# Start addresses of the operands that TensorE streams, in a float32r kernel of three transformer layers

## The chip, the core and the metric

The kernel runs on one core of a Trainium2 chip. The metric is the device time of one execution in microseconds. The median of 3 runs of the kernel before is 2257.28 us (2252.32 to 2262.8).

## The reference

A sequence of 512 positions with 1024 features goes through three residual layers, all in float32: retention with 4 heads and a squared-ReLU MLP of width 4096; attention over chunks of 64 with 16 heads and a relative bias, and a second such MLP; and a hybrid layer. Cut to what matters:

```python
h = h + _retention(rmsnorm(h), ret_w_in, ret_gn_g, ret_w_out)
h = h + relu(rmsnorm(h) @ mlp_w1[0]) ** 2 @ mlp_w2[0]
h = h + _chunk_attention(rmsnorm(h), att_w_in, att_rel_bias, att_w_out)
h = h + relu(rmsnorm(h) @ mlp_w1[1]) ** 2 @ mlp_w2[1]
x = rmsnorm(h)
z = rmsnorm(x) @ w_in            # q, k, v of three attentions, a forget gate, three gates
merged = sigmoid(ga) * (o_a @ w_pa) + sigmoid(gb) * (o_b @ w_pb) + sigmoid(gc) * (o_c @ w_pc)
x = x + merged @ w_o
a, b = split(causal_dwconv(rmsnorm(x) @ w_up))
return rmsnorm(x + (silu(a) * b) @ w_down)
```

Nearly all of the arithmetic is products of the 512 positions with weight matrices.

## The kernel before, in words

Everything is kept feature-major: a tile is 128 features by 512 positions, and the residual `h` is 8 such tiles. The weights come as a stream of 358 units of 128 x 1024 float32 (512 KB each), most of them eight blocks of 128 x 128, in the order in which the products need them. SyncE loads unit after unit into the ring `raw` of four slots. ScalarE rounds a unit to float32r into `w_hi` (line 952), VectorE puts the rest, raw minus w_hi, into `w_lo` (line 1376), both three units ahead of the products. The activations are split likewise: `x_hi` and `x_lo` hold the 8 tiles of a layer's input, and `arena_r`, 29 tiles of 512 float32r, holds every other split operand: q, k, v and probabilities, attention outputs, the MLP's hidden tiles, the products of the gated unit. `arena` holds 17 tiles of plain float32 scratch.

A product of two float32 numbers is made of three float32r products, written in the helper `mm3`, whose three lines are 487, 488 and 489 in the profile:

```python
(lh, ll), (rh, rl) = left, right
pe.matmul(dst, lh, rh, start=start, stop=False, **kw)
pe.matmul(dst, lh, rl, start=False, stop=False, **kw)
return pe.matmul(dst, ll, rh, start=False, stop=stop, **kw)
```

```
tensor            bytes each   before: start, past a multiple of 2048
w_hi, w_lo        16384        32896, 49280     128
x_hi, x_lo        16384        82048, 98432     128
h, rbc, sq, acc, diag          65664 to 127104  128
arena             34816        133952           832
arena_r           59392        168768           832
```

A slice of these that TensorE streams starts a multiple of 512 bytes further on, a whole tile a multiple of 2048.

Of the kernel before, what the change touches and what calls it, by code (L numbers as in the profile page):

```python
# [23 lines left out]
F32R = mybir.dt.float32r  # L24
# [3 lines left out]
P = 128  # L28
S = 512
D = 1024  # L30
KT = D // P
# [4 lines left out]
UNIT = 1024  # L36
RING = 4
# [14 lines left out]

NORMS, BOTH = 7, 4
STRIP = 640

# [5 lines left out]
N_COLS = C_CB + 2 * PAIRS  # L63
# [114 lines left out]
def wait(eng, sem, count):  # L178

    count = lin(count)  # L180
    assert count.b > 0 or not count.a, count.b
    if count.positive():
        eng.wait_ge(sem, count.val())

def build(nc, stream, x_t, cols, wf, f_bias, sinks, rel_pad, rel_2, c_rope, c_decay, c_sq, c_tri, c_sel,
          c_onehot, c_masked, out):

    strips = nc.dram_tensor("bias_strips", (12, P, STRIP), F32, kind="Internal").ap()
    with ExitStack() as ctx:  # L190
        def sb(name, shape, dt=F32):
            return ctx.enter_context(nc.sbuf_tensor(name, shape, dt))
# [2 lines left out]
            return ctx.enter_context(nc.semaphore(name))  # L195

        raw = sb("raw", [P, RING, UNIT])
        w_hi = sb("w_hi", [P, RING, UNIT], F32R)
        w_lo = sb("w_lo", [P, RING, UNIT], F32R)
        h = sb("h", [P, KT, S])  # L200
        x_hi = sb("x_hi", [P, KT, S], F32R)
        x_lo = sb("x_lo", [P, KT, S], F32R)
        rbc = sb("rbc", [P, S])
        sq = sb("sq", [P, 4, S])
        acc = sb("acc", [P, S])
        diag = sb("diag", [P, TT, P])
        ident = sb("ident", [P, P])
        ones = sb("ones", [P, P])
        sqr = sb("sqr", [P, 3, P], F32R)
        colv = sb("colv", [P, N_COLS])  # L210
        small = sb("small", [P, 12, 16])
        wf_raw = sb("wf_raw", [P, KT, 4])
        wf_hi = sb("wf_hi", [P, KT, 4], F32R)
        wf_lo = sb("wf_lo", [P, KT, 4], F32R)
        rel_sb = sb("rel_sb", [BUCKETS + 2, 12])
        arena = sb("arena", [P, 17 * S])
        arena_r = sb("arena_r", [P, 29 * S], F32R)

        banks = [ctx.enter_context(nc.psum_tensor(f"bank{n}", [P, S], F32)) for n in range(8)]

# [175 lines left out]

        onehot_sb = arena[0:BUCKETS + 2, 8 * S:8 * S + STRIP]
        strip_sb = arena[0:12, 10 * S:10 * S + STRIP]
        masks_sb = arena[:, 12 * S:12 * S + 3 * P].rearrange("p (m n) -> p m n", m=3)
# [1518 lines left out]
        def _(pool):  # L1918
# [35 lines left out]
            pool.wait_ge(strip_copied, 1)  # L1954
            pool.dma_start(strips, strip_sb.unsqueeze(1).broadcast_to([12, P, STRIP])).then_inc(strip_saved, 16)

# [44 lines left out]
            def toeplitz(sm, hd, table, row, offset, w):  # L2001

                wait(pool, sm.biased, 4 * (hd - 1) if hd >= 2 else 0)
                src = bass.AP(table.tensor, row * P * STRIP + offset + P - 1, [[STRIP - 1, P], [1, w]])
                pool.dma_start(bias[hd % 2][:, 0:w], src).then_inc(sm.bias[hd % 2], 16)
# [65 lines left out]
def bucket_table():  # L2072

    f = np.float32
    ahead = 511 - np.arange(STRIP)
    dist = np.maximum(ahead, 0)
# [162 lines left out]
```

## Time and profile before

| | before |
|---|---|
| median of 3 runs | 2257.28 us |
| the profiled execution, span from first to last instruction | 2256.0 us |
| TensorE busy | 98% of the span |
| VectorE, ScalarE, GpSimd busy | 53%, 36%, 11% |
| mean granted TensorE clock | 0.983 |

The profiled execution has no time of its own beside its span; the span is 1.3 us under the median of the runs, within their spread. Matmuls are pipelined: one starts before the one before it has ended, so the mean duration of a matmul in the rows is longer than the distance from start to start, and the sum of the groups' times exceeds the span. What one product costs TensorE is to be read from the starts. The clock is given as a share of full speed: 1.0 is the 2.4 GHz level, 0.5 the 1.2 GHz level.

### The profile page before, as it was taken

The page shows a single profiled execution, that of the slowest core. Times are in us where ns is not written, and L with a number is a line of the kernel's source. Part 1 is how long each engine was busy: PE and PEld are TensorE (multiplying, and loading weights), DVE is VectorE, ACT ScalarE, POOL GpSimd, SP SyncE. Part 2 cuts the span into 40 slices and gives each one's busy share as a digit, 9 for nine tenths or more (in the row PEclk, how much of TensorE's full clock was granted, in tenths as well). Part 3 has the DMA queues.
Part 4 walks back from the last instruction along what each step waited for, and adds up shares of the span by engine and source line. Part 5 has one row for each costly group of instructions (what it writes and reads, how often), then busy time and mean ns, then how long its engine had stood idle before and what let it go on. Part 6 is the DMA issues. An engine that isn't in the chain of part 4 may idle for free.

```text
span 2256.0 us, 27545 instructions
## 1 busy us (share of the span) xinstructions
PE 2205.0 (98%) x9956; PEld 1797.2 (80%) x9956; DVE 1199.6 (53%) x1757; ACT 814.2 (36%) x1303; POOL 259.0 (11%) x312
## 2 busy tenths in 40 slices
PE   7899999899999999999999999999999999999997
PEld 5788888688888878888888888877887878888885
DVE  5364555563454544666634535554545455656674
ACT  4333342432222334565322223344453234433342
POOL 3222231300000011222000000211210000000001
PEclk9999999999999999999999999998999999999998
DMA  7532323132323332222233223321213322333332
GB/s 190 114 102 72 100 60 102 56 94 94 98 90 98 97 103 84 75 70 71 93 94 94 92 94 94 106 66 32 66 54 94 97 90 93 103 112 110 96 105 91
DMA packets 58124, 205.52 MB, mean 91 GB/s; under 512 B 7061, under 2 KB 7205, under 8 KB 58048
## 3 DMA queue, kind: packets, MB, share of 16 engines
q1 hardware_dynamic: 52704, 189.82, 27.1%
q0 software_dynamic: 3760, 11.92, 2.8%
q10 hardware_dynamic: 1584, 2.75, 0.3%
q8 instruction: 50, 0.82, 0.2%
q14 instruction: 26, 0.21, 0.0%
HBM read 198.43 MB, written 6.03 MB: 91 GB/s over the span
## 4 chain that ended last, share of the span: by engine, by line
PE 93%; DVE 3%; ACT 1%; DMA 1%; issue 1%; POOL 0%; ACTq 0%; POOLq 0%; DVEq 0%; SPq 0%
PE bank L487 30%; PE bank L488 30%; PE bank L489 30%; PE bank L705 2%; DMA raw<-in_stream 1%; DVE w_lo L1376 1%; ACT w_hi L952 1%; DVE h L1426 0%; PE bank L553 0%; PE bank L541 0%; POOL arena_r L1961 0%; PE bank L540 0%; DVE x_lo L1382 0%; PE bank L690 0%; DVE h L1913 0%
## 5 line engine op out<-in xcount | busy, mean ns | idle before, releaser
L487 PE MATMUL bank<-x_hi,w_hi 128*128 128x512 f32 x1552 | 620.9, 400 | 5.4 <-DVE x_lo L1382 2.8
L1376 DVE TENSOR_TENSOR w_lo<-raw,w_hi 128x1024 fp32r<-128x1024 f32 x358 | 465.4, 1301 | 298.3 <-ACT w_hi L952 297.6
L488 PE MATMUL bank<-x_lo,w_hi 128*128 128x512 f32 x1552 | 609.3, 393 | 0.0
L489 PE MATMUL bank<-x_hi,w_lo 128*128 128x512 f32 x1552 | 608.9, 392 | 0.0
L952 ACT ACTIVATE w_hi<-raw 128x1024 fp32r<-128x1024 f32 x358 | 376.2, 1053 | 437.1 <-PE bank L489 411.3
L487 PE MATMUL bank<-arena_r,w_hi 128*128 128x512 f32 x1008 | 399.7, 397 | 12.2 <-POOL arena_r L1961 7.3
L489 PE MATMUL bank<-arena_r,w_lo 128*128 128x512 f32 x1008 | 397.9, 395 | 0.0
L488 PE MATMUL bank<-arena_r,w_hi 128*128 128x512 f32 x1008 | 397.9, 395 | 0.0
L487 PEld LDWEIGHTS bank<-x_hi,w_hi 128*128 128x128 f32 x1552 | 295.0, 190 | 72.8 <-DVE x_lo L1382 5.5
L488 PEld LDWEIGHTS bank<-x_lo,w_hi 128*128 128x128 f32 x1552 | 295.0, 190 | 62.5 <-issue 3.1
L489 PEld LDWEIGHTS bank<-x_hi,w_lo 128*128 128x128 f32 x1552 | 294.4, 190 | 63.1
L487 PEld LDWEIGHTS bank<-arena_r,w_hi 128*128 128x128 f32 x1008 | 188.9, 187 | 64.5 <-issue 12.2
L1426 DVE TENSOR_TENSOR h<-bank,h 128x512 f32<-128x512 f32 x152 | 104.6, 689 | 239.4 <-PE bank L489 239.3
L489 PEld LDWEIGHTS bank<-arena_r,w_lo 128*128 128x128 f32 x1008 | 189.0, 187 | 46.7
L488 PEld LDWEIGHTS bank<-arena_r,w_hi 128*128 128x128 f32 x1008 | 189.0, 188 | 45.2
L1421 DVE TENSOR_TENSOR arena<-bank,rbc 128x512 f32<-128x512 f32 x125 | 86.3, 690 | 171.8 <-PE bank L489 164.3
L1107 ACT ACTIVATE arena_r<-arena 128x512 fp32r<-128x512 f32 x64 | 40.5, 632 | 247.4 <-DVE arena L1578 247.4
L487 PE MATMUL bank<-arena_r 128*128 128x256 f32 (+5 forms) x352 | 114.8, 326 | 10.5 <-DVE arena_r L1506 8.4
L489 PE MATMUL bank<-arena_r 128*128 128x256 f32 (+5 forms) x352 | 112.5, 320 | 0.0
L488 PE MATMUL bank<-arena_r 128*128 128x256 f32 (+5 forms) x352 | 112.3, 319 | 0.0
L1934 POOL TENSOR_TENSOR acc<-sq 128x512 f32<-128x512 f32 x6 | 8.3, 1389 | 872.3 <-ACT sq L964 518.4
L1998 POOL TENSOR_SCALAR arena<-arena,small 128x256 f32<-128x256 f32 (+3 forms) x128 | 65.0, 521 | 344.5 <-DVE small L1633 285.7
(203 smaller groups left out, 2010.8 us busy)
## 6 DMA issues: line engine op xcount, KB each, us to landing
raw<-in_stream SPq DMA_DIRECT2D x358, 512.0 KB, 3.5
arena<-in_rel_pad POOLq DMA_DIRECT2D x16, 256.0 KB, 3.0
bias_strips<-arena POOLq DMA_DIRECT2D x1, 3840.0 KB, 56.6
h<-in_x_t ACTq DMA_DIRECT2D x8, 256.0 KB, 6.1
out_t<-h SPq DMA_DIRECT2D x8, 256.0 KB, 2.2
arena<-in_c_decay POOLq DMA_DIRECT2D x4, 256.0 KB, 3.1
arena<-bias_strips POOLq DMA_DIRECT2D x4, 256.0 KB, 3.7
arena<-bias_strips POOLq DMA_DIRECT2D x8, 128.0 KB, 2.4
```

Of the source, the lines that this page charges most:

```text
L487: pe.matmul(dst, lh, rh, start=start, stop=False, **kw)
L488: pe.matmul(dst, lh, rl, start=False, stop=False, **kw)
L489: return pe.matmul(dst, ll, rh, start=False, stop=stop, **kw)
L705: m = pe.transpose(banks[b][:, o + (t - j) * P:o + (t - j) * P + P], pf[par][:, src:src + P], ident[:, :])
L952: act.activation(w_hi[:, u % RING, :], raw[:, u % RING, :], ACT.Copy).then_inc(hi_ready, 1)
L1107: act.activation(uh[j], uf[j % 2], ACT.Copy).then_inc(u_hi, 1)
L1376: dve.tensor_tensor(w_lo[:, s, :], raw[:, s, :], f32(w_hi[:, s, :]), ALU.subtract).then_inc(lo_ready, 1)
L1421: return dve.tensor_tensor(dst, banks[(at.t - 1) % 2][:, :], rbc[:, :], ALU.mult)
L1426: dve.tensor_tensor(h[:, j, :], banks[(at.t - 1) % 2][:, :], h[:, j, :], ALU.add).then_inc(tile_read, 1)
L1934: pool.tensor_tensor(acc[:, :], sq[:, 0, :], sq[:, 1, :], ALU.add).then_inc(acc_sum, 1)
L1998: pool.tensor_scalar(pf[par][:, a:a + w], pf[par][:, a:a + w], rinv[par][:, t:t + 1], 1.0, ALU.mult, ALU.mult).then_inc(sm.probs, 1)
```

## The change

The allocations are put in another order, with a pad of 240 floats (960 bytes). No instruction changes.

```diff
 NORMS, BOTH = 7, 4
+PAD = 240
 STRIP = 640
...
         raw = sb("raw", [P, RING, UNIT])
-        w_hi = sb("w_hi", [P, RING, UNIT], F32R)
-        w_lo = sb("w_lo", [P, RING, UNIT], F32R)
         h = sb("h", [P, KT, S])
-        x_hi = sb("x_hi", [P, KT, S], F32R)
-        x_lo = sb("x_lo", [P, KT, S], F32R)
         rbc = sb("rbc", [P, S])
         sq = sb("sq", [P, 4, S])
         acc = sb("acc", [P, S])
         diag = sb("diag", [P, TT, P])
+        arena = sb("arena", [P, 17 * S])
         ident = sb("ident", [P, P])
         ones = sb("ones", [P, P])
         sqr = sb("sqr", [P, 3, P], F32R)
-        colv = sb("colv", [P, N_COLS])
-        small = sb("small", [P, 12, 16])
         wf_raw = sb("wf_raw", [P, KT, 4])
         wf_hi = sb("wf_hi", [P, KT, 4], F32R)
         wf_lo = sb("wf_lo", [P, KT, 4], F32R)
         rel_sb = sb("rel_sb", [BUCKETS + 2, 12])
-        arena = sb("arena", [P, 17 * S])
+
+        sb("pad", [P, PAD])
+        w_hi = sb("w_hi", [P, RING, UNIT], F32R)
+        w_lo = sb("w_lo", [P, RING, UNIT], F32R)
+        x_hi = sb("x_hi", [P, KT, S], F32R)
+        x_lo = sb("x_lo", [P, KT, S], F32R)
         arena_r = sb("arena_r", [P, 29 * S], F32R)
+        colv = sb("colv", [P, N_COLS])
+        small = sb("small", [P, 12, 16])
```

With the sizes added up, `w_hi` starts at byte 102,400, which is 50 x 2048, and `w_lo`, `x_hi`, `x_lo` and `arena_r` follow it, each at a multiple of 2048, since each is a whole number of 2048 bytes long. `raw`, `h`, `rbc`, `sq`, `acc`, `diag` and `arena` are 128 past a multiple of 2048; for all but `arena` that is as before.

## Rows read from the trace of the kernel before

**Rows 1.** Page, part 1: busy us, share of the span, instructions, by engine.
```profile
PE 2205.0 (98%) x9956; PEld 1797.2 (80%) x9956; DVE 1199.6 (53%) x1757; ACT 814.2 (36%) x1303; POOL 259.0 (11%) x312
```

**Rows 2.** Page, part 4: chain that ended last, by engine and by line.
```profile
PE 93%; DVE 3%; ACT 1%; DMA 1%; issue 1%; POOL 0%; ACTq 0%; POOLq 0%; DVEq 0%; SPq 0%
PE bank L487 30%; PE bank L488 30%; PE bank L489 30%; PE bank L705 2%; DMA raw<-in_stream 1%; DVE w_lo L1376 1%; ACT w_hi L952 1%; DVE h L1426 0%; PE bank L553 0%; PE bank L541 0%; POOL arena_r L1961 0%; PE bank L540 0%; DVE x_lo L1382 0%; PE bank L690 0%; DVE h L1913 0%
```

**Rows 3.** Groups by shape, TensorE: count | busy us, mean ns of one | idle before.
```profile
L487 PE MATMUL bank<-x_hi,w_hi 128*128 128x512 f32 x1552 | 620.9, 400 | 5.4 <-DVE x_lo L1382 2.8 <-DVE w_lo L1376 1.3 <-DVE arena L1465 0.7
...
L487 PE MATMUL bank<-arena_r,w_hi 128*128 128x512 f32 x1008 | 399.7, 397 | 12.2 <-POOL arena_r L1961 7.3 <-DVE h L1426 2.6 <-DVE arena L1808 1.8
...
L487 PE MATMUL bank<-w_hi,x_hi 128*128 128x512 f32 x224 | 87.6, 391 | 0.9 <-ACT arena L1191 0.9
...
L487 PE MATMUL bank<-arena_r 128*128 128x256 f32 x72 | 21.6, 300 | 10.5 <-DVE arena_r L1506 8.4 <-DVE arena_r L1628 2.1
...
L487 PE MATMUL bank<-arena_r 128*128 128x512 f32 x48 | 19.4, 405 | 0.0
...
L487 PE MATMUL bank<-arena_r 128*128 128x384 f32 x48 | 16.1, 335 | 0.0
```

**Rows 4.** Timeline, TensorE, three edges of MLP blocks: start us, duration us, instruction.
```profile
1342.06 0.39 PE L487 MATMUL bank<-x_hi,w_hi 128*128 128x512 f32 x1
...
1385.60 0.39 PE L487 MATMUL bank<-arena_r,w_hi 128*128 128x512 f32 x1
...
1430.39 0.39 PE L487 MATMUL bank<-x_hi,w_hi 128*128 128x512 f32 x1
```

**Rows 5.** Stretches: length, busy PE, PEld, DVE, ACT, POOL, granted clock, DMA share, GB/s.
```profile
1438.80:1443.00 4.20, 4.20 (x11) 3.25 (x10) 0.91 (x3) 0.21 (x1) 0.00 (x0) 0.50 0.45 174
1342.00:1385.60 43.60, 43.60 (x194) 36.05 (x194) 25.03 (x30) 12.15 (x15) 0.00 (x0) 1.00 0.28 85
1385.60:1430.40 44.80, 44.80 (x194) 35.91 (x193) 25.33 (x24) 21.23 (x30) 15.26 (x12) 1.00 0.30 94
```

**Rows 6.** Timeline, TensorE, a stretch at the lower clock.
```profile
1438.75 0.63 PE L488 MATMUL bank<-x_lo,w_hi 128*128 128x512 f32 x1
...
1443.02 0.63 PE L489 MATMUL bank<-x_hi,w_lo 128*128 128x512 f32 x1
```

**Rows 7.** Timeline, TensorE, the two instructions of one product of line 553.
```profile
1084.31 0.59 PE L553 MATMUL bank<-diag,ones 128*128 128x512 f32 x1
...
1084.74 0.59 PE L553 MATMUL bank<-diag,ones 128*128 128x512 f32 x1
```

**Rows 8.** Timeline, TensorE, retention scores, six products of each width.
```profile
281.58 0.39 PE L487 MATMUL bank<-arena_r 128*128 128x512 f32 x1
...
282.97 0.33 PE L487 MATMUL bank<-arena_r 128*128 128x384 f32 x1
...
284.04 0.28 PE L487 MATMUL bank<-arena_r 128*128 128x256 f32 x1
...
284.74 0.22 PE L487 MATMUL bank<-arena_r 128*128 128x128 f32 x1
```

**Rows 9.** Page, part 5: VectorE's split of the weights.
```profile
L1376 DVE TENSOR_TENSOR w_lo<-raw,w_hi 128x1024 fp32r<-128x1024 f32 x358 | 465.4, 1301 | 298.3 <-ACT w_hi L952 297.6
```

**Rows 10.** Span and mean granted clock of the core.
```profile
core 0: 2256.0 us, clock 0.983
```

**Rows 11.** Chain of waits up to 78 us, longest piece: start us, us, what.
```profile
43.63 28.98 DMA raw<-in_stream
```

**Rows 12.** Stretches, columns as in rows 5: the start, and the chunk attention.
```profile
0.00:76.00 76.00, 56.64 (x226) 42.88 (x226) 38.41 (x42) 28.73 (x40) 22.14 (x24) 0.95 0.79 177
...
882.00:1046.00 164.00, 163.23 (x884) 138.60 (x883) 106.10 (x276) 95.57 (x243) 45.64 (x88) 1.00 0.24 71
```

**Rows 13.** Chain of waits from 2190 to 2240 us, one unit of the last `down`.
```profile
2227.32 1.06 ACT w_hi L952
2228.39 1.54 DVE w_lo L1376
```

## Prediction

> **What bounds the kernel now.** I read the busy shares first: TensorE has 98% of the span, VectorE 53%, ScalarE 36% [rows 1]. A busy TensorE can still be waiting inside, so I went on to the chain of waits. It runs through TensorE for 93% of the span, nearly all of it through the three lines of `mm3`, 487 to 489 [rows 2]. So the time is, to a first order, the number of products times the time from the start of one to the start of the next. The groups by shape give the number. With a moving operand 512 columns wide there are 1552 × 3 products that stream x_hi or x_lo, 224 × 3 that stream w_hi or w_lo (names swapped, token-major), and 1008 × 3 that stream arena_r against w [rows 3]: 5328 and 3024. Their "mean ns of one", 390 to 400, is no cost, since one starts before the last ends. The cost is the distance of starts, from the timeline.
>
> An MLP block of TensorE's work is 8 units of 24 products, 192, without a gap. One that streams x runs from 1342.06 to 1385.60: 43.54 us, **226.8 ns** each. The next streams arena_r, from 1385.60 to 1430.39: 44.79 us, **233.3 ns** each [rows 4]. The stationary side is w_hi and w_lo in both, the shape is the same, the granted clock is 1.00 in both (the 2.4 GHz level) and nothing waits [rows 5]. What differs is the tensor that streams, and where it starts: x and w lie 128 bytes past a multiple of 2048 and of 256, arena_r 832 bytes past one of 2048, which is 64 past one of 256. So something about the moving operand's place costs 6.5 ns a product. I take the start address as the likeliest reading; that arena_r lies higher in the partition is the other one.
>
> Is 226.8 itself too much? Two stretches say so. With the granted clock at 0.50 (the 1.2 GHz level) [rows 5], ten x products start from 1438.75 to 1443.02, 427 ns apart [rows 6]: at twice the speed that is 213.5. And a full-precision product of diag, line 553, also 128 past a multiple of 2048, has 430 ns between its two instructions [rows 7], at full clock. Twice 215 is what it would be if each makes two passes over the 512 columns, which is my reading. So 13 ns of an x product and 20 ns of an arena_r product appear only when columns are streamed once, at full clock. The extra grows with width: the arena_r products at 281.58 take 232 ns for 512 columns (six in 1.39 us), 178 for 384 (six in 1.07) and 117 for 256 (six in 0.70) [rows 8], against 213.5, 160 and 107. A collision with the 128-column weight load, or a charge per instruction, would be about the same at each width. It is a property of the stream, and that speaks for the address.
>
> **The change, part by part.** No instruction, wait, queue or order changes; only addresses. Three effects.
>
> First, w_hi, w_lo, x_hi and x_lo go from 128 past a multiple of 2048 to a multiple. The trace has no single-pass stream at such an address, so I bound the new distance. From below: 213.5, half the 427. From above: the linear continuation of the two addresses shown, 64 past costs 233.3 and 128 past 226.8, so 0 past could cost 239.8. Between lies "unchanged", 226.8. I take 216: nearest to it is line 553's 215, and I add 1 because there a weight load comes once in 1024 columns and not once in 512. That gives 10.8 ns × 5328 = 57.5 us. The Trainium skill ("TensorE: Matmul & The Clock Gate", Back-to-back issue gap) gives N/2.4 + 2.5 ns, 215.7 for 512 columns. The trace does not agree for this kernel, with 226.8 and 233.3; by the page, the sum would be 8352 × 0.3 ns = 2.5 us larger.
>
> Second, arena_r goes from 832 past to 0: 233.3 − 216 = 17.3 ns × 3024 = 52.3 us. Its products with itself follow [rows 3, 8]: 48 × 3 of 512 columns × 17 ns = 2.4 us, 48 × 3 of 384 from 178 to 163 = 2.2 us, 72 × 3 of 256 from 117 to 109 = 1.7 us. The fewer shapes of 64 rows and the 128-column ones, which sit under their weight loads, I leave out.
>
> Third, arena, h, sq, diag and the others move by whole multiples of 2048, save arena (832 to 128 past), colv, small, ident, ones, sqr, wf and rel_sb. VectorE, ScalarE and GpSimd read and write these. I cost that at nothing: VectorE's split takes 1.30 us [rows 9] and ScalarE's 1.06 [rows 13] for each unit of 24 × 226.8 ns = 5.44 us, so even a tenth more would be hidden by TensorE. Uncovered, over 358 splits a tenth more on VectorE would be 47 us. DMAs keep their sizes.
>
> Sum: 57.5 + 52.3 + 6.3 = 116.1 us. Four deductions. (a) The mean granted clock is 0.983 [rows 10], so about 3.4% of the time is at half clock, where x products already take 427: 4 us. (b) Up to 76 us the chain follows the weight stream: one stretch of 28.98 us is the load of raw [rows 11], with DMA at 0.79 [rows 12]. The 226 products there save nothing: 2.4 us. (c) The last `down` has units of 12 products, 2.8 us, and there the chain returns to the splits, 1.06 + 1.54 us a unit [rows 13]; 96 × 17.3 ns = 1.7 us. (d) In the attention stage, 882 to 1046, TensorE is full (163.2 of 164 us) but VectorE has 106 and ScalarE 96 [rows 12]. As TensorE gets faster a softmax link may be late next; 3 us. Together 11, so **105 us** off. What is late next is the stream at the start and the splits at the end; in the middle VectorE, at 25 of 44 to 45 us, has room [rows 5]. The profiled execution's span is 2256.0, 1.3 us under the median of the runs, 2257.3, so I take the gain off the median: **2152 us**.
>
> **Rivals.**
> *Part of the way* (chance 0.15). Address helps, but a floor of the stream remains, say at 220 ns: 6.8 × 5328 + 13.3 × 3024 + 4 = 80 us, less 8, so 2185. For it: the two addresses differ by only 6.5 of 20 ns. Against: line 553 shows no floor above 215.
>
> *128 bytes were enough* (0.18). The extra 13 ns is what a single-pass stream costs anywhere, and only arena_r was badly placed. Then arena_r gets 226.8: 6.5 × 3024 + 2 = 22 us, less 1, so 2236. For it: line 553 reads its data at half the rate, so it may hide what a full-rate stream can't. Against: nothing else.
>
> *It isn't the address* (0.13). The 6.5 ns belong to arena_r's height or to something unseen, and nothing moves: 2257, within 2252 to 2263. The Trainium skill ("SBUF — State Buffer", cachelines) knows a penalty for lines of 16 bytes, and by it this would be the outcome, since 128 and 832 are both multiples of 16 already. That the trace has two speeds at two such addresses does not agree with it as a whole account.
>
> *Nearer to the boundary is dearer* (0.12). The line through the two points goes on: 64 bytes closer costs 6.5 ns more, at 0 the distance is 239.8. That is 13 × 5328 + 6.5 × 3024 + 3 = 92 us more: 2349. Its place is every product; it decides as soon as the new mean distance is above today's, (5328 × 226.8 + 3024 × 233.3) / 8352 = 229.2 ns. For it: two points fit any line, and 64 → 128 went in the good direction. Against: the extra per product is 13.3 and 19.8 ns, a ratio of 2 to 3, which a distance of 2 and 3 blocks of 64 bytes to the next multiple of 256 explains, but at 0 that distance is as well none as four; none seems the more natural.
>
> **How the numbers follow.** The forecast case gets 0.42. With 213.5 for 216 it gains 8352 × 2.5 ns = 21 us more, about 2131, and 2128 if the deductions are smaller; with ten more us lost to splits and softmax, 2162. The range of 8 in 10 must take that case, "part of the way", "128 bytes" and "not the address", 0.88 together; without the last it is 0.75 and too little. So 2128 to 2262. The case's own range is 2128 to 2162. A measurement can tell about 0.5%, 11 us. Faster by that: 0.42 + 0.15 + 0.18, less a little for a small gain that gets lost, 0.72. Same: 0.13 plus that, less a little, 0.15. Slower: 0.12 and a point for what I don't see, 0.13.
>
> **What the profile will show.** The MLP blocks of 192 products decide: both kinds in 41.5 us (216 ns) if right; both in 43.5 for "128 bytes"; 43.5 and 44.8 for "not the address"; 46.0 for "dearer". The half-clock stretches stay at 427, line 553 at 430. TensorE's busy time falls to about 2100, the chain stays on lines 487 to 489 with a larger share of VectorE and of the load of raw. It is wrong if x and arena_r blocks still differ, if the blocks reach 41.5 but the span falls by less than 90 us (then a wait I didn't see took it), or if VectorE's or ScalarE's groups change their mean by over 3%.

## The result and the profile after

The changed kernel takes **2234.8 us** (median of 4 runs, 2233.87 to 2235.57) against 2257.4 before: ratio 0.9899, 95% interval 0.9881 to 0.9916. That is 22.6 us less, where 105 were forecast. The direction was right and the size was not; the rival "128 bytes were enough" had said 2236.

The busy shares and the chain by engine of the page after, which answer to [rows 1, 2]:

```profile
PE 2180.3 (98%) x9956; PEld 1796.4 (80%) x9956; DVE 1198.7 (54%) x1757; ACT 814.4 (36%) x1303; POOL 258.4 (12%) x312
...
PE 93%; DVE 3%; DMA 1%; ACT 1%; issue 1%; ACTq 0%; POOL 0%; POOLq 0%; DVEq 0%; SPq 0%
```

TensorE lost 24.7 us of busy time; VectorE's and ScalarE's work cost what it did (VectorE's split of the weights has a mean of 1300 ns, 1301 before). So the gain is inside the products. The same three edges of MLP blocks as in [rows 4], from the timeline after (the lines of the code are 3 further down):

```profile
1335.46 0.39 PE L490 MATMUL bank<-x_hi,w_hi 128*128 128x512 f32 x1
...
1378.98 0.39 PE L490 MATMUL bank<-arena_r,w_hi 128*128 128x512 f32 x1
...
1422.50 0.39 PE L490 MATMUL bank<-x_hi,w_hi 128*128 128x512 f32 x1
```

The x block takes 43.52 us, 226.7 ns a product, where it took 43.54: **nothing changed for it**. The arena_r block takes 43.52 us where it took 44.79: 226.7 ns instead of 233.3. Over 3024 products that is 3024 × 6.6 = 20.0 us. The products of arena_r with itself gave about 1 us more. Six of 512 columns, the same retention scores as in [rows 8], now take 1.36 us where they took 1.39, that is 226.7 ns each and not 232:

```profile
285.38 0.39 PE L490 MATMUL bank<-arena_r 128*128 128x512 f32 x1
...
286.74 0.33 PE L490 MATMUL bank<-arena_r 128*128 128x384 f32 x1
```

The rest of TensorE's 24.7 us belongs to the clock. Two pairs of stretches with about the same work, before and then after (columns as in rows 5):

```profile
0.00:44.84 44.84, 32.28 (x118) 22.83 (x119) 28.97 (x32) 21.06 (x30) 19.59 (x22) 0.96 0.78 205
1430.40:1460.00 29.60, 29.60 (x126) 24.03 (x125) 14.30 (x22) 7.84 (x11) 3.45 (x5) 0.88 0.37 116
```

```profile
0.00:48.90 48.90, 35.83 (x118) 25.98 (x119) 29.07 (x32) 21.05 (x30) 19.57 (x22) 0.86 0.78 195
1422.50:1452.50 30.00, 30.00 (x142) 24.55 (x141) 17.59 (x25) 8.90 (x12) 3.83 (x6) 1.00 0.37 115
```

The first 118 products took 4.1 us longer after the change, with a granted clock of 0.86 instead of 0.96; behind the MLP the clock stood at 1.00 instead of 0.88, and 142 products fitted into the time of 126. Such stretches came and went between the runs below, whatever the placement (the mean granted clock of the full kernels' runs lies between 0.981 and 0.989), and I read nothing into them. In all the trace has 76.9 us at half clock before and 69.0 after, which is worth 4 us. So 20.0, 1 and 4 us make up the 24.7 within the rounding; against that TensorE stood idle for 52.8 us and not 51.0, which leaves the 22.9 us between the spans.

### The profile page after: what moved, and what is told of

Its sections match the earlier page's. It is cut to its first block, busy times and chain, and to the rows that moved or that the text cites. A ratio compares the mean times of both kernels' runs of the same rounds, so it can differ in the third digit from the quotient of the medians.

```text
span 2233.1 us, 27545 instructions
## 1 busy us (share of the span) xinstructions
PE 2180.3 (98%) x9956; PEld 1796.4 (80%) x9956; DVE 1198.7 (54%) x1757; ACT 814.4 (36%) x1303; POOL 258.4 (12%) x312
## 4 chain that ended last, share of the span: by engine, by line
PE 93%; DVE 3%; DMA 1%; ACT 1%; issue 1%; ACTq 0%; POOL 0%; POOLq 0%; DVEq 0%; SPq 0%
PE bank L490 30%; PE bank L491 30%; PE bank L492 30%; PE bank L708 2%; DMA raw<-in_stream 1%; DVE w_lo L1379 1%; ACT w_hi L955 1%; DVE h L1429 0%; PE bank L544 0%; PE bank L556 0%; PE bank L543 0%; DVE x_lo L1385 0%; PE bank L693 0%; DVE h L1916 0%; PE bank L839 0%
## 5 line engine op out<-in xcount | busy, mean ns | idle before, releaser
L490 PE MATMUL bank<-arena_r,w_hi 128*128 128x512 f32 x1008 | 395.2, 392 | 12.9 <-POOL arena_r L1964 7.0
L491 PE MATMUL bank<-arena_r,w_hi 128*128 128x512 f32 x1008 | 393.2, 390 | 0.0
L492 PE MATMUL bank<-arena_r,w_lo 128*128 128x512 f32 x1008 | 393.1, 390 | 0.0
L490 PE MATMUL bank<-arena_r 128*128 128x256 f32 (+5 forms) x352 | 113.7, 323 | 10.8 <-DVE arena_r L1509 8.8
```

## The experiments

At first sight the result is the rival's: arena_r was badly placed, 128 bytes are enough, and 226.7 ns is what a float32r stream costs. I called that theory A and tested it against the theories and rivals that the expectations below name. Starts are given in bytes past a multiple of 2048.

**arena_only.** Is the rest of the change needed?

```diff
         arena = sb("arena", [P, 17 * S])
+        sb("pad", [P, 16])
         arena_r = sb("arena_r", [P, 29 * S], F32R)
```

> The kernel before with a pad of 64 bytes ahead of arena_r alone, which then starts at 896 past a multiple of 2048, a multiple of 128; w and x stay at 128 past, arena at 832. Theory A (a start at a multiple of 128 bytes is enough): arena_r blocks of 192 products take 43.5 us, and the time is that of the changed kernel, 2235, ratio to before 0.990. Rival D (the start must be a multiple of 256 or more, or moving and stationary operand must share their place modulo 2048): 44.8 us and 2257. Rival E (arena's move from 832 to 128 helped too): between the two, by some us.

Measured: 2238.0 us, ratio to before 0.9914 (0.9899 to 0.993). The timeline:

```profile
1378.91 0.39 PE L488 MATMUL bank<-arena_r,w_hi 128*128 128x512 f32 x1
...
1422.43 0.39 PE L488 MATMUL bank<-x_hi,w_hi 128*128 128x512 f32 x1
```

43.52 us again. Sixty-four bytes ahead of one tensor do what the whole change does. Rival D falls in both of its forms as they were put: no start here is a multiple of 2048, and arena_r (896) and w (128) don't share their place modulo 2048. That they do share it modulo 256 I had not seen yet. Rival E, a gain from arena's own move, has little room: the interval overlaps that of the changed kernel, and all_64 below, which has arena moved as well, took 2236.0, 2 us less.

**all_64.** Theory A's plainest forecast: put everything where arena_r was.

```diff
-PAD = 240
+PAD = 256
```

> The changed kernel with 64 bytes more pad: w, x and arena_r all start 64 past a multiple of 2048. Theory A: every product of 512 columns takes 233.3 ns, both kinds of MLP blocks 44.8 us; 5328 + 3024 products x 6.6 ns = 55 us more than the changed kernel, about 2288. Rival D in its form of sharing the place modulo 2048: 226.7 and 2235.

Measured: 2236.0 us, ratio 0.9909 (0.9888 to 0.9929). Nothing got slower:

```profile
1335.65 0.39 PE L490 MATMUL bank<-x_hi,w_hi 128*128 128x512 f32 x1
...
1379.17 0.39 PE L490 MATMUL bank<-arena_r,w_hi 128*128 128x512 f32 x1
...
1422.69 0.39 PE L490 MATMUL bank<-x_hi,w_hi 128*128 128x512 f32 x1
```

Both blocks take 43.52 us with arena_r 64 bytes past a multiple of 256, exactly as before the change. **Theory A is wrong, and the rival that hit the number had the wrong reason.** The start of the moving operand by itself decides nothing.

**w_64.** Here w stands 64 bytes below the two others.

```diff
-PAD = 240
+PAD = 256
...
         w_lo = sb("w_lo", [P, RING, UNIT], F32R)
+        sb("pad_2", [P, 16])
         x_hi = sb("x_hi", [P, KT, S], F32R)
```

> The changed kernel with w_hi and w_lo 64 past a multiple of 2048, x_hi, x_lo and arena_r 128 past. Theory A (only the moving operand counts): only the 672 products that stream w, the token-major ones, take 233.3 ns, 672 x 6.6 ns = 4.4 us more than the changed kernel, 2239; MLP blocks stay at 43.5 us. Rival F (the stationary operand's start counts as well): the MLP blocks rise too, up to 44.8 us, and the time up to 2288.

Measured: 2255.2 us, ratio 0.999 (0.9979 to 1.0001). Theory A had said 2239. The moving operands are better aligned than in all_64, and the kernel is 19 us slower:

```profile
48.62 0.39 PE L491 MATMUL bank<-w_hi,x_hi 128*128 128x512 f32 x1
...
71.01 0.39 PE L491 MATMUL bank<-arena_r 128*128 128x512 f32 x1
...
1346.55 0.39 PE L491 MATMUL bank<-x_hi,w_hi 128*128 128x512 f32 x1
...
1390.50 0.39 PE L491 MATMUL bank<-arena_r,w_hi 128*128 128x512 f32 x1
...
1434.44 0.39 PE L491 MATMUL bank<-x_hi,w_hi 128*128 128x512 f32 x1
```

Both kinds of blocks now take 43.95 and 43.94 us, 228.9 ns a product, and the 96 token-major products from 48.62 to 71.01 take 233.2. So the stationary operand's place counts (rival F), together with the moving one's. That the total is that of the kernel before is a coincidence: there 3024 products paid 6.6 ns, here 7680 pay 2.2 and 672 pay 6.6.

**micro_offsets.** This kernel leaves out all of the computation and lets TensorE work alone.

```diff
+            for n in range(N):
+                m = pe.matmul(bank[:, :], w[:, n % 4 * P:n % 4 * P + P], s[:, 16:16 + S], start=True, stop=True)
...
```

> This kernel leaves out everything of the computation and copies x to the output; TensorE alone runs series of 24 products of 128x128 with 512, 384, 256 or 128 columns, each series with its moving operand at another number of bytes past a multiple of 2048, float32r and bfloat16. Theory A (only the lower bits of the moving operand's start count, 128 bytes are enough, and 226.7 ns is what a float32r stream of 512 columns costs): 226.7 ns at 0, 128, 256, 384, 512 and 1024; 233.3 at 64, 192, 320 and 832; bfloat16 near 216 at every start; nothing changes with the stationary operand's start or width. Theory B (the 13 ns above 213.5 come from the work of other engines, from DMA or from the weight load): here, with the others idle, 214 to 216 at 0, or with a stationary operand of 64 columns. Theory C (the distance to the next multiple of 256 counts): 192 lies between 213.5 and 226.7, and 0 and 256 alike.

Its timeline has one row per series: start, duration, instruction, count. The start of the next series minus this one's, by 24, is the distance of starts. The lines stand for the place of the moving operand: 59 for 0, 61 for 16, 67 for 64, 69 for 96, 71 for 128, 73 for 160; then bfloat16, 113 for 0, 115 for 32, 117 for 64.

```profile
38.39 5.60 PE L59 MATMUL bank<-s,w 128*128 128x512 f32 x24
43.83 5.72 PE L61 MATMUL bank<-s,w 128*128 128x512 f32 x24
...
60.59 5.67 PE L67 MATMUL bank<-s,w 128*128 128x512 f32 x24
66.09 5.77 PE L69 MATMUL bank<-s,w 128*128 128x512 f32 x24
71.70 5.76 PE L71 MATMUL bank<-s,w 128*128 128x512 f32 x24
77.30 5.78 PE L73 MATMUL bank<-s,w 128*128 128x512 f32 x24
...
174.32 5.35 PE L113 MATMUL bank<-sbf,wbf 128*128 128x512 bf16 x24
179.51 5.34 PE L115 MATMUL bank<-sbf,wbf 128*128 128x512 bf16 x24
184.69 5.34 PE L117 MATMUL bank<-sbf,wbf 128*128 128x512 bf16 x24
```

That gives 226.7 ns at 0, 229.2 at 64 and 233.3 at 128; 192, not shown, is as 128. With the stationary operand at 64 the list turns: 233.3 for a moving start of 0, 227.5 for 64. Theory B falls: the other engines are idle and 226.7 stays, so neither they nor DMA make it, and with a stationary operand of 64 columns the series took 230 ns and not 214 to 216. Starts off the 16-byte grid were no better: 236.6 ns at 4 bytes and 233.2 at 8. Theory A falls again: 128 is worse than 64. Theory C falls too: 192 is among the worst. And bfloat16 takes 216 ns ((184.69 − 179.51) / 24) at all four starts tried.

**The new theory, G.** With w at 0 here, the cost goes with the moving start: 0, 64, 128, 192 give 226.7, 229, 233.3, 233.3. The products that have w on one side fit the same list in all full kernels so far, if one takes the moving start minus the stationary one, modulo 256. Before: x minus w is 0, arena_r minus w is 832 − 128 = 704, which is 192. In w_64, x and arena_r minus w is 64, and w minus x, for the token-major products, 192. In arena_only, all_64 and the changed kernel every difference is 0.

One group does not fit, and I had passed over it. The products of arena_r with itself have a difference of 0 in every kernel, the one before included, since slices of one tensor lie multiples of 512 bytes apart. By the list they take 226.7 ns and can't gain. Yet the scores in [rows 8] took 232 ns, behind products of arena_r with w that paid for a difference of 192. In the changed kernel, arena_only and all_64, where the products ahead of them are at 0 too, all four retention heads' scores take 226.7. The absolute place isn't it: in all_64 arena_r is 64 past a multiple of 256, as in the kernel before. So what a product costs depends also on what ran before it.

Theory G is that the stream of a product collides in SBUF with the weight load that runs beside it, and that the difference modulo 256 says how much. Three further kernels tested it.

**micro_pairs.** All pairs of four starts.

> This kernel leaves out everything of the computation and copies x to the output; TensorE alone runs series of 72 products whose moving and stationary operands start at chosen bytes past a multiple of 256. Theory G (the stream of a product collides with the weight load of the next one, and what counts is the moving operand's start minus the stationary one's, modulo 256): 226.7 ns wherever the two are alike, 229 at +64, 233.5 at +128, 233.3 at +192, whatever the absolute starts; pages of the difference above 256 don't matter, so every fixed stationary start from 256 to 65536 gives 226.7. If the 13 ns that are left at difference 0 are a collision too, they shrink with fewer stationary columns (64: half) and stay the same for fewer moving columns (384: 173.4, 256: 120). Theory H (absolute starts count): rows with the same difference differ. Theory I (the 13 ns belong to the float32r stream): unchanged with 4 stationary columns.

Measured, eight of the sixteen series, by lines: 59 to 65 have the stationary operand at 0 and the moving one at 0, 64, 128 and 192; 67 to 73 have the stationary operand at 64 and the moving one at the same four.

```profile
66.61 16.48 PE L59 MATMUL bank<-s,w 128*128 128x512 f32 x72
82.93 16.66 PE L61 MATMUL bank<-s,w 128*128 128x512 f32 x72
99.43 16.90 PE L63 MATMUL bank<-s,w 128*128 128x512 f32 x72
116.17 16.95 PE L65 MATMUL bank<-s,w 128*128 128x512 f32 x72
132.96 16.96 PE L67 MATMUL bank<-s,w 128*128 128x512 f32 x72
149.76 16.50 PE L69 MATMUL bank<-s,w 128*128 128x512 f32 x72
166.10 16.66 PE L71 MATMUL bank<-s,w 128*128 128x512 f32 x72
182.59 16.89 PE L73 MATMUL bank<-s,w 128*128 128x512 f32 x72
```

The durations form the same list, turned by one place: 16.5, 16.66, 16.9, 16.95 at stationary 0 for moving 0, 64, 128, 192, and the same four at stationary 64 for moving 64, 128, 192, 0. In steady state the distances are 226.7, 228.9, 232.3 and 233.3 ns for differences of 0, 64, 128 and 192, and the other eight series repeat them within 0.3. Theory H, that absolute starts count, is out for these four. Steady state takes a while: the first distances of the series at L69, which has a difference of 0 and follows one at 192, are 225, 236, 229, 232, 231 and 227 ns. A run of six products, as in rows 8, ends before it has settled. Nine stationary starts from 256 to 65536 bytes further on all gave 226.7: nothing above 256 matters. Finer steps, with the moving operand at 0: a stationary start of 16 or 240 was as good as 0, while 32, 96, 160 and 224 cost 233.3 to 234.2. Here the rule has a hole: a stationary start of 240 and a moving start of 16 are the same difference, and the first took 226.7 ns, the second 231.4 (in micro_offsets). So the difference is a rule for steps of 64 bytes, not for steps of 16.

The last part asked whose the remaining 13 ns are. Rows of 384 and 256 columns at difference 0, 256 at 192, then 512 columns with 64 and with 4 stationary columns:

```profile
578.84 12.67 PE L121 MATMUL bank<-s,w 128*128 128x384 f32 x72
...
629.21 8.78 PE L129 MATMUL bank<-s,w 128*128 128x256 f32 x72
...
654.86 8.35 PE L135 MATMUL bank<-s,w 128*128 128x256 f32 x72
...
761.68 16.72 PE L153 MATMUL bank<-s,w 128*64 128x512 f32 x72
778.24 16.60 PE L155 MATMUL bank<-s,w 128*64 128x512 f32 x72
...
894.58 16.84 PE L169 MATMUL bank<-s,w 128*4 128x512 f32 x72
911.26 16.84 PE L171 MATMUL bank<-s,w 128*4 128x512 f32 x72
```

At difference 0 the distances are 226.7, 173.3 and 120.0 ns for 512, 384 and 256 columns: 53.3 a step of 128 columns, which is 2.4 GHz to the digit, and the same 13.3 on top of each. There it is a charge per product, not one that grows. Elsewhere it does grow: at difference 192 the same three widths cost 20.0, 16.6 and 6.6 ns over their columns. At 256 columns a difference of 192 is the best (113.3) and 0 the worst.

The list also holds for a full stationary operand only. For differences of 0, 64, 128 and 192 the distances are 230.0, 233.4, 231.7 and 228.3 ns with 96 stationary columns, and 230.1, 228.4, 229.4 and 232.8 with 64. At difference 0 a narrower load is therefore dearer: 226.7 with 128 columns, 230.1 with 64, (911.26 − 894.58) / 72 = 231.7 with 4, where the difference no longer matters. So half of theory G's second part held and half did not: the charge stays with fewer moving columns, but a shorter load does not reduce it. Theory I has "unchanged with 4 columns" only roughly right (231.7 for 226.7).

**apart_128.** Full kernel, every difference 128, all moving starts of x and arena_r at multiples of 256.

```diff
+        sb("pad", [P, 32])
         x_hi = sb("x_hi", [P, KT, S], F32R)
...
+        sb("pad_2", [P, 16])
         arena_r = sb("arena_r", [P, 29 * S], F32R)
```

> The kernel before with pads that put x at 256 and arena_r at 1024 past a multiple of 2048, w stays at 128: every difference is 128 modulo 256, though x and arena_r are better aligned than before. Theory G: 233.5 ns for both kinds of MLP blocks (44.8 us) and for the token-major products, 8352 x 6.7 ns = 56 us over the changed kernel, about 2291, slower than before by some 1.5%. Theory H (a multiple of 256 is best): 226.7 or less and 2235.

Measured: 2281.9 us, ratio to before **1.0104** (1.0081 to 1.0126). The timeline:

```profile
1361.74 0.39 PE L489 MATMUL bank<-x_hi,w_hi 128*128 128x512 f32 x1
...
1406.35 0.40 PE L489 MATMUL bank<-arena_r,w_hi 128*128 128x512 f32 x1
...
1450.98 0.39 PE L489 MATMUL bank<-x_hi,w_hi 128*128 128x512 f32 x1
```

44.61 and 44.63 us, 232.4 ns a product. Better aligned operands made the kernel slower than before. The forecast of 2291 used 233.5 from the short series; with 232.4, 8352 × 5.7 = 48 us over the changed kernel is 2283.

**x_192.** x pays in full and arena_r a third of it.

```diff
+        sb("pad", [P, 48])
         x_hi = sb("x_hi", [P, KT, S], F32R)
...
+        sb("pad_2", [P, 48])
         arena_r = sb("arena_r", [P, 29 * S], F32R)
```

> The kernel before with x at 320 and arena_r at 1216 past a multiple of 2048, w stays at 128: x minus w is 192, arena_r minus w is 64 modulo 256, w minus x is 64. Theory G: x blocks 44.8 us, arena_r blocks 43.95 (228.9 ns), token-major products 228.9; 4656 x 6.6 + 3696 x 2.2 ns = 39 us over the changed kernel, about 2274. Theory H: by x at 320 and arena_r at 1216, both 64 modulo 128, 233.3 everywhere and 2288.

Measured: 2276.0 us, ratio 1.0077 (1.0051 to 1.0102).

```profile
1358.08 0.39 PE L489 MATMUL bank<-x_hi,w_hi 128*128 128x512 f32 x1
...
1402.87 0.39 PE L489 MATMUL bank<-arena_r,w_hi 128*128 128x512 f32 x1
...
1446.82 0.39 PE L489 MATMUL bank<-x_hi,w_hi 128*128 128x512 f32 x1
```

The x block takes 44.79 us and the arena_r block 43.95, as theory G said: x is now the dear one. Theory H had said 2288 and 233.3 for both. One thing was off, the token-major products. All have a difference of 64. These are the starts of the 96 products of the first retention head and of whatever follows them, then the same for the second head:

```profile
49.41 0.39 PE L489 MATMUL bank<-w_hi,x_hi 128*128 128x512 f32 x1
...
71.40 0.39 PE L489 MATMUL bank<-arena_r 128*128 128x512 f32 x1
...
142.38 0.40 PE L489 MATMUL bank<-w_hi,x_hi 128*128 128x512 f32 x1
...
164.77 0.39 PE L489 MATMUL bank<-arena_r,w_hi 128*128 128x512 f32 x1
```

The first 96 take 229.1 ns each and the second 233.2, and both keep their distance to the end. Heads three and four are like the second; in the attention the first half is at 233.3 and the second at 229.0. The same pair of places can settle at two speeds, then, and what ran before seems to decide which: the list is what a pair mostly costs, not a law. In the long MLP blocks of the seven full kernels it held each time.

**micro_triples.** Is there a placement better than all alike?

> This kernel leaves out everything of the computation and copies x to the output; TensorE alone runs 64 series of 24 triples in the order of mm3 (w_hi with x_hi, w_hi with x_lo, w_lo with x_hi), with w_hi at a multiple of 256 and the three others each 0, 64, 128 or 192 past one. Theory G (each product costs by its moving start minus the stationary start that is loaded meanwhile, and by nothing else): the mean of a triple is the mean of three values among 226.7, 228.9, 232.3 and 233.3; all alike, 226.7, is the least, and no series is under it. Theory J (the collision has a memory, so that mixed places can dodge it): some series lie under 226.7, down to 220, and then there is a placement that beats the changed kernel, by up to 8352 x 6.7 = 56 us.

Measured, the first product of a series and of the one behind it: all alike (line 59), then w_lo 192, x_hi 0, x_lo 192 (line 263):

```profile
65.98 0.39 PE L59 MATMUL bank<-s,w 128*128 128x512 f32 x1
...
82.30 0.39 PE L63 MATMUL bank<-s,w 128*128 128x512 f32 x1
...
916.36 0.39 PE L263 MATMUL bank<-s,w 128*128 128x512 f32 x1
...
933.15 0.40 PE L267 MATMUL bank<-s,w 128*128 128x512 f32 x1
```

All alike has 226.7 ns a product and is the least of the 64. The next one (w_lo 0, x_hi and x_lo 64) has 228.9, the middle of the field 231.2, the worst 235.6. So no placement of this grid beats the changed kernel, and theory J's hope is gone. But theory G's "by nothing else" fell too. The series at line 263 has differences to the next load of 0, 0 and 0 and takes 233.2 ns; its two sisters with 128 and with 64 in place of 192 take 231.1. Over all 64 series the mean of three values from the list misses the measured one by 2.1 ns on the average, while always saying 231.2 misses it by 1.3. For mixed sequences the list says nothing, except that all alike is best. Nor does it show that it is the next load that counts: pairing each stream with its own stationary operand misses by 2.0 ns.

## Why the prediction was right or wrong

**What bounds the kernel** was right: TensorE's products, and a change of a few ns in their distance goes to the end nearly undiminished. Of the 22.6 us, 3024 × 6.6 = 20 us are the products of arena_r with w.

**The second effect, arena_r,** was right in that it was badly placed and would gain, and wrong in size: 6.6 ns of the 17.3 came, since the goal of 216 was wrong.

**The first effect was the step that failed**: "10.8 ns × 5328 = 57.5 us" was 0. The new distance was put at 216 ns, and it measured 226.7, what x products had taken all along. x and w shared their place modulo 256 before the change and after it. With 216 gone, 57.5 us there, 3024 × 10.7 = 32 us of arena_r's 52.3 and most of the 6.3 us of its own products go too, while the deductions of 11 us that went with them were not needed in full.

Two readings led there. *The address as an absolute number*: the trace showed two moving starts, 128 and 832, against one stationary start, 128. Both "64 or 128 past a multiple of 256" and "difference 0 or 192" fit these. I even had the stationary side in view and noted that it was w in both blocks, and took that as a reason to leave it out; a constant in the difference is not outside of it. *"The extra grows with width"*: I took 18, 18 and 10 ns of [rows 8] as growth, though between 384 and 512 columns there was none, and with it dismissed the collision with the weight load. Measured by itself at difference 0, the charge is 13.3 ns at 512, 384 and 256 columns. Rows 8 come from runs of six products behind dearer ones, which had not settled. The dismissal was wrong: the stationary operand, which only the weight load reads, decides with its place what the stream costs. That the two reads collide, and how, remains a reading; no run shows it.

**The floors of 215 and 213.5** were no likeness. Line 553 and the bfloat16 series (216) have next to no charge, the float32r products have one. And at half clock the charge and the effect of places are both absent: x products take 427 ns there at difference 0 (before), 128 (apart_128) and 192 (x_192), which is 512 columns at 1.2 GHz and nothing more. Half of that is not what the full clock gives. The Trainium skill ("TensorE: Matmul & The Clock Gate", Back-to-back issue gap) and its N/2.4 + 2.5 ns, about 216 for 512 columns, agree with the bfloat16 series here, 216, and not with float32r, 226.7.

**The rivals.** "128 bytes were enough" had the place, the block time and the total (2236 for 2234.8), and a false reason: all_64 has neither w, x nor arena_r at a multiple of 128 and is as fast. That its number came true was luck. "Part of the way" was right that a floor remains; it is at 226.7 and not at 220, so x gained nothing. "Nearer to the boundary is dearer" was false. "It isn't the address" was false, and the 16-byte lines of the Trainium skill ("SBUF — State Buffer", cachelines) do not account for it: every placement of the full kernels is a multiple of 16, and they differ by up to 6.7 ns a product. The same page (Who interferes with whom) gives TensorE two independent read ports, one for the stream and one for weight loads, and says that TensorE waits on no one. The ports may well be two. But w_64 and micro_pairs show that the place of what one reads changes the pace of the other, by up to 6.7 ns in 233, with every other engine idle in micro_pairs.

**Other work** cost nothing, as said: VectorE's and ScalarE's means moved by 1 ns.

**What stays open:** what repeats every 256 bytes, why 32 bytes off is as bad as 192, and what carries over from one product to the next, so that one pair of places settles at 229 or at 233 ns. Open too is the owner of the 13.3 ns that all alike still pays, by estimate 8352 × 13.3 = 111 us of this kernel: a load of 4 columns in place of 128 did not lower it, another engine's work does not cause it, and products without any weight load between them were not tried.

## What to carry to other kernels

When float32r products of 512 columns with a full stationary operand of 128 columns bound a kernel, place the moving and the stationary tensors at the same offset modulo 256 bytes; here that is worth up to 6.7 ns in 233, and pads of 64 or 128 bytes decide 1% either way. For narrower operands measure first: with 256 moving columns, or 64 or 96 stationary ones, another difference was the best. Don't align for its own sake: apart_128 aligned better and lost 1%. Where a trace shows one operand in two places, ask what the other operand does before calling it a rule about one address, and measure such a thing in a repeated series with nothing else going on.

## What was not expected of the hardware

- In long series of one pair the distance of float32r products goes by moving minus stationary start modulo 256: 226.7, 228.9, 232.3 and 233.3 ns for 0, 64, 128 and 192, with 512 moving and 128 stationary columns, for all sixteen pairs of starts; bfloat16 takes 216 at all four moving starts tried.
- At difference 0 a product costs 13.3 ns over its columns at 2.4 GHz, for 256, 384 and 512 columns alike. At half clock x products take 427 ns, with no such charge, at differences of 0, 128 and 192.
- The order depends on both widths: with 256 moving columns it is 120.0 ns at difference 0 and 113.3 at 192; with 96 stationary columns 192 is the best (228.3), with 64 it is 64 (228.4).
- The cost has a memory. Scores at difference 0 took 232 ns in the kernel before and 226.7 in the changed one; 96 products at difference 64 ran at 229.1 ns once and at 233.2 another time in one kernel; in mixed sequences the costs are not those of the pairs.
